# The last tile of an output projection in pieces, the shift of rows moved to GpSimd, and one weight load issued earlier

## What is computed

```python
x = x + g1 * y_x                                        # y_x = (merged branches) @ w_out
hx2 = modulate(rms_norm(x, norm_ffn_g[l]), sh2, sc2)    # h * (1 + scale) + shift
x = x + g2 * grouped_moe(hx2, router_w, router_b, w_exp_gate[l], w_exp_up[l], w_exp_down[l])

# grouped_moe
scores = jax.nn.sigmoid((h @ router_w).astype(jnp.float32))
biased = scores + router_b.astype(jnp.float32)
group_score = lax.top_k(grouped, TOP_K)[0].sum(-1)      # 4 groups of 4 experts, the best group wins
_, idx = lax.top_k(masked, TOP_K)                       # two experts within it
for e in range(N_EXPERTS):
    he = jax.nn.silu(h @ w_gate[e]) * (h @ w_up[e])
    out = out + combine[..., e:e + 1] * (he @ w_down[e])
```

## Time and profile before

| | us |
|---|---|
| median of 3 runs | 1580.73 |
| range of the runs | 1579.6 to 1580.88 |
| the profiled execution, its own time | 1578.25 |
| its span (first to last instruction) | 1576.6 |
| PE busy | 1506.4 (96%) |
| DVE busy | 704.4 (45%) |
| ACT busy | 332.8 (21%) |
| POOL busy | 118.8 (8%) |

### The profile page before, as it was taken

One profiled execution on the slowest core, in us unless ns is written; L12 is line 12 of the kernel. 1 busy time (PEld: TensorE's weight loads), 2 busy tenths in 40 slices (PEclk: granted clock), 3 DMA queues, 4 the chain that ended last, 5 costly groups with the idle time before them and its releaser, 6 DMA issues. The chain is left out here.

```text
span 1576.6 us, 23833 instructions
## 1 busy us (share of the span) xinstructions
PE 1506.4 (96%) x9898; PEld 1023.3 (65%) x9898; DVE 704.4 (45%) x1420; ACT 332.8 (21%) x769; POOL 118.8 (8%) x101
## 2 busy tenths in 40 slices
PE   5999999999999999899999999999999999899995
PEld 2765644766677768775546648786678887655563
DVE  1497777577775442732221135336534312512122
ACT  2121244322223110210101023225322211100001
POOL 0100000032212210000000030000000000000000
PEclk9999999999999999999999999999999999999998
DMA  9575411333544589489999984431134376899997
GB/s 372 203 239 166 156 54 43 119 133 124 158 147 160 173 286 358 173 322 391 400 394 392 402 314 147 138 97 45 38 111 146 121 283 266 343 426 428 419 411 296
DMA packets 128364, 370.24 MB, mean 235 GB/s; under 512 B 14269, under 2 KB 91351, under 8 KB 107516
## 3 DMA queue, kind: packets, MB, share of 16 engines
q1 hardware_dynamic: 118588, 344.86, 58.8%
q10 hardware_dynamic: 5936, 13.09, 2.3%
q0 software_dynamic: 3728, 10.71, 1.9%
HBM read 361.66 MB, written 12.98 MB: 238 GB/s over the span
## 5 line engine op out<-in xcount | busy, mean ns | idle before, releaser
L1247 PE MATMUL ps<-hT,ring 128*128 128x512 f32 (+1 forms) x544 | 207.6, 535 | 0.0
L1250 PE MATMUL ps<-ring,hT 128*128 128x256 f32 (+1 forms) x832 | 173.1, 364 | 3.7 <-DVE arena L2242 2.3
L1250 PEld LDWEIGHTS ps<-ring,hT 128*128 128x128 f32 x832 | 147.0, 190 | 27.5 <-issue 10.3
L1247 PEld LDWEIGHTS ps<-hT,ring 128*128 128x128 f32 x544 | 101.3, 191 | 86.9 <-issue 81.7
L1446 PE MATMUL ps<-arena,ring 128*128 128x512 f32 (+1 forms) x384 | 136.3, 486 | 0.0
L1596 PE MATMUL ps<-arena 128*32 128x128 f32 (+2 forms) x1104 | 102.4, 342 | 0.7 <-DVE arena L2554 0.7
L1596 PE MATMUL ps<-ring,arena 128*64 128x256 f32 (+1 forms) x1280 | 93.9, 334 | 3.8 <-DMA ring<-in_w_exp_gate 2.1
L1446 PEld LDWEIGHTS ps<-arena,ring 128*128 128x128 f32 x384 | 72.4, 190 | 31.7 <-issue 24.6
L2856 POOL DMA_INDIRECT arena<-moe_rows,idx_i x23 | 22.8, 991 | 897.8 <-DVE idx_i L2622 512.9
L1381 PE MATMUL ps<-hT,ring 128*128 128x256 f32 x384 | 87.9, 379 | 0.6 <-ACT arena L1903 0.6
L1159 PE MATMUL ps<-ring,arena 128*128 128x256 f32 x384 | 85.9, 380 | 2.5 <-DVE arena L2420 2.5
(11 more groups left out here) (310 smaller groups left out, 1962.5 us busy)
## 6 DMA issues: line engine op xcount, KB each, us to landing
ring<-in_w_in SPq DMA_DIRECT2D x54, 1024.0 KB, 6.2
ring<-in_w_ada SPq DMA_DIRECT2D x48, 1024.0 KB, 5.3
arena<-in_w_exp_down SPq DMA_DIRECT2D x18, 2048.0 KB, 16.1
arena<-in_w_exp_up SPq DMA_DIRECT2D x15, 2048.0 KB, 15.8
ring<-in_w_exp_down SPq DMA_DIRECT2D x14, 2048.0 KB, 13.7
ring<-in_w_exp_gate SPq DMA_DIRECT2D x12, 2048.0 KB, 16.4
ring<-in_w_exp_up SPq DMA_DIRECT2D x12, 2048.0 KB, 15.0
hT<-in_w_exp_gate SPq DMA_DIRECT2D x10, 2048.0 KB, 15.7
```

The lines of the kernel that those rows point to most:

```text
L1247: last = pe.matmul(ps[:, bank, 0:tok.stop - tok.start], w[:, k, at:at + width], hT[:, k, tok], start=(k == 0), stop=(k == KD - 1))
L1250: last = pe.matmul(ps[:, bank, 0:width], hT[:, k, P * tok:P * (tok + 1)], w[:, k, at:at + width], start=(k == 0), stop=(k == KD - 1))
```

## The change

It has nine parts; the same code serves both layers, so all but the last act twice.

1. The last tile's second half of `w_out` is counted after each quarter. The second quarter goes to the other PSUM bank. DVE mixes 256 columns at a time (`mix(..., piece)`).
2. The first 256 of these columns are turned within the second quarter's product (before its last two steps, `turn_last(0)`), the other 256 after six of the eight router steps (`turn_last(1)`). DVE copies them in two pieces (`keep_last`).
3. The last tile's squares are made over 768 columns and then over 256. The mean of the first part enters the root as its bias (`mean_of_most`).
4. Two small activations call the square root's table and the sigmoid's table ahead of their use.
5. DVE, not ACT, copies the last tile's router strips (`keep_last_parts`).
6. `shift_rows` of all tiles but the last moves to GpSimd. `scale_rows` of these writes into the place of the next tile's row, and its second half for the last but one tile stands behind the first piece of the last tile's mix.
7. The last tile's shift stays on DVE, in halves: column blocks 0 to 3 at its old place, blocks 4 to 7 behind the marks of the slots. PE waits for the first half ahead of the first rows and for the second ahead of column block 4.
8. `keep_busy` has 14 products instead of 10, and three more stand around the last router steps.
9. In the last layer SP issues the gate of expert 2 ahead of the row of tile 3, as the first layer already does.

```diff
-BUSY = (10, 10)
+BUSY = (14, 14)
...
                 first_expert(2)
                 sp.wait_ge(logits, 2 * before(nq, l + 1))
-                if l == 0:
-                    expert_tile(l, 2, 0, 2)
+                expert_tile(l, 2, 0, 2)
                 rows_out(NT - 1)
...
+                            if ends and quarter:
+                                pe.wait_ge(x_mixed, v + l)
+                            bank = 4 + (v + (ends and quarter)) % 2
+                            for k in range(KD):
+                                if ends and quarter and k == KD - 2:
+                                    turn_last(0)
...
-                turn_x(NT - 1, 1)
                 add_parts(NT - 2)
-                router(NT - 1)
+                router(NT - 1, range(6))
+                turn_last(1)
+                keep_busy(2, 1)
+                router(NT - 1, range(6, KD))
+                keep_busy(1, 1)
                 add_parts(NT - 1)
                 keep_busy(BUSY[l])
...
+                mix(NT - 1, 1, 0)
+                keep_x(NT - 2)
+                scale_rows(NT - 2, 1)
+                mean_of_most()
+                keep_last(0)
+                mix(NT - 1, 1, 1)
+                if NT - 3 >= t0:
+                    scale_logits(NT - 3)
+                keep_last(1)
+                scale_logits(NT - 2)
+                keep_last_parts()
+                dve.wait_ge(x_mixed, halves(l, 2 * nq[l] + 1))
+                root_of(NT - 1)
+                scale_rows(NT - 1, 0)
+                scale_logits(NT - 1)
+                scale_rows(NT - 1, 1)
...
-                shift_rows(NT - 1)
+                shift_last(0)
...
                 dve.tensor_tensor(next_slots[:, 0:n, :].rearrange("p t (a q) -> p t a q", a=lists),
...
+                shift_last(1)
...
+            def shift_rows(l, t):
+
+                by_row = lambda a: a.rearrange("p (q k) -> p q k", k=KD)
+                if t > first_tile(l):
+                    pool.wait_ge(h2_ready, turned_halves(l, t - first_tile(l)))
+                pool.wait_ge(consts_made, scalings(l, t - first_tile(l) + 1))
+                pool.tensor_tensor(h_toks[l][:, t, :].rearrange("p (k q) -> p q k", k=KD), by_row(rows_scaled(l, t)),
+                                   by_row(ffn_rows[l][t // XT][1]), ALU.add).then_inc(h2_ready, 1)
```

More of the change, by code:

```diff
@@ L498, in trunk, with scalings, halves, turned_halves @@
         nq = [NT - first_tile(l) for l in range(DEPTH)]
+        def scalings(l, n):
+            return CONSTS + before(nq, l) + n
+        def halves(l, n):
+            return 2 * before(nq, l) + l + n
+        def turned_halves(l, n):
+            return before(nq, l) + l + n
         def roots(l, n):
@@ L830, in multiplied @@
             if kind == "out":
-                return wo_ready, 2 * before(nq, l) + nq[l] * (1 + j // 2)
+                return wo_ready, halves(l, nq[l] * (1 + j // 2) + j // 2)
             return (moe.gate, moe.up, moe.down)[j], EXPERTS * l + max(i for i in range(EXPERTS) if i % WAYS[l][j] == 0) + 1
@@ L1141, in _ @@
                 sp.nop()
-            sp.wait_ge(x_mixed, 2 * before(nq, DEPTH))
-            sp.wait_ge(h2_ready, before(nq, DEPTH))
+            sp.wait_ge(x_mixed, halves(DEPTH, 0))
+            sp.wait_ge(h2_ready, turned_halves(DEPTH, 0))
             sp.wait_ge(moe.gate, EXPERTS * DEPTH - 2)
@@ L1475, in _, with turn_last @@
                         mods_turn(*at)
+                def turn_last(piece):
+                    pe.wait_ge(x_mixed, halves(l, 2 * nq[l] + piece))
+                    if piece:
+                        pe.wait_ge(h2_dve, turned_halves(l, 1))
+                    else:
+                        pe.wait_ge(h2_act, 2 * before(nq, l) + nq[l])
+                    for k in range(2):
+                        last = pe.transpose(ps[:, 0 if piece else nq[l] - 1, P * k:P * (k + 1)],
+                                            res[:, NT - 1, P * (4 + 2 * piece + k):P * (5 + 2 * piece + k)], ident)
+                    last.then_inc(h2_turned, 1)
                 def turn_x(t, half):
-                    pe.wait_ge(x_mixed, 2 * before(nq, l) + nq[l] * half + t - t0 + 1)
+                    pe.wait_ge(x_mixed, halves(l, nq[l] * half + t - t0 + 1))
                     if half:
@@ L1521, in _ @@
                         v = 2 * before(nq, l) + nq[l] * half + t - t0
+                        ends = half and t == NT - 1
                         if v >= 2:
-                            pe.wait_ge(x_mixed, v - 1)
+                            pe.wait_ge(x_mixed, v - 1 + l)
                         for quarter in range(2):
@@ L1531, in _ @@
                             w = kview(n_out + 2 * half + quarter)
-                            last = product(ps[:, 4 + v % 2, COLS * quarter:COLS * (quarter + 1)],
-                                           [(yT[l][k][:, P * t:P * (t + 1)], w[:, k, :]) for k in range(KD)])
+                            if ends and quarter:
[4 more added lines that the diff above has]
+                                    turn_last(0)
+                                last = pe.matmul(ps[:, bank, COLS * quarter:COLS * (quarter + 1)], yT[l][k][:, P * t:P * (t + 1)],
+                                                 w[:, k, :], start=(k == 0), stop=(k == KD - 1))
+                            if ends and not quarter:
+                                last.then_inc(wo_ready, 1)
                         last.then_inc(wo_ready, 1)
@@ L2001, in keep_parts @@
                     act.activation(parts_kept[:, i % 2, :], ps[:, 6, P * i:P * (i + 1)], ACT.Copy).then_inc(h2_act, 1)
+                act.activation(root[:, :], eps[:, :], ACT.Sqrt)
                 for t in range(t0, NT):
@@ L2006, in _ @@
                 for t in range(t0, NT):
-                    squares(ready, junk2, t, t + 1)
+                    if t == NT - 1:
+                        squares_of_most()
                     if t > t0:
                         keep_parts(t - 1)
-                keep_parts(NT - 1)
+                    if t < NT - 1:
+                        squares(ready, junk2, t, t + 1)
+                squares_of_last()
+                act.activation(root[:, :], eps[:, :], ACT.Sigmoid)
                 act.wait_ge(scaled, before(nq, l + 1))
@@ L2536, in _ @@
                         scale_logits(t - 2)
-                    if t == NT - 1:
-                        keep_x(t)
-                        scale_logits(t - 1)
-                        dve.wait_ge(x_mixed, 2 * before(nq, l + 1))
-                    dve.wait_ge(std_ready, roots(l, NT + t - t0 + 1))
-                    step(dve.reciprocal(rstd[:, t:t + 1], rstd[:, t:t + 1]))
+                    root_of(t)
                     if t == t0:
```

115 lines of the change are left out of this document (77 added, 38 removed).

## The result

The changed kernel takes 1584.48 us (median of 16 runs, 1582.43 to 1588.41), the kernel before 1580.88 beside it: ratio 1.0020, 95% interval 1.0013 to 1.0028. It is slower by 3.6 us where the forecast was 6.9 us of gain.

The account below looks back on a forecast made before the run. PE's waits were taken to bound the kernel first, in the last layer the weight stream. Terms 0.9 + 1.3 + 3.2 + 1.5 = 6.9 us gave 1573.8 us against the median of 1580.73; range 1570.5 to 1578.8.

Parts of the forecast that it names:

- the wait gone: First layer, up to the last tile: PE's wait for keep_x at 638.47 disappears, 0.9 us gained.
- the last tile: First layer, last tile: assign ready 0.5 us earlier and the marks 0.8 us earlier still, 1.3 us gained.
- The clock term: First layer: full clock under the first half of the first expert's rows, 3.2 us; rival of low clock 0.27.
- arrives at the end unchanged: What the first layer's passage gives PE was claimed to reach the end in full.
- PE's chain: Last layer: first rows at 1348.4 instead of 1351.31, expert 0's gate done 2.9 us earlier for PE.
- GpSimd's shift: Last layer: tile 2's shift on GpSimd taken as 3.7 us, so its row goes 1.95 us later.
- The lower bound: Last layer: the least time taken for GpSimd's shift of tile 2, 2.35 us.
- DVE is slowed by GpSimd: Rival, both layers: one slowed DVE step in each costs 1.0 us; about 1578.5, no measurable change; chance 0.10.
- I take 7: Last layer: expert 1's gather assumed to land in 7 us, between 4.9 on idle queues and 8.3 on full ones.
- The term of +1.5: Last layer, weight stream: 1.5 us gained by filling idle DMA time, bounds −0.4 and 3.2.
- the third gate costs the gather: Rival, last layer: gather as slow as 8.3 us, term −0.4, sum 5.0, 1575.7 us; chance 0.12.

Follow-up runs that it names:

- e1: The changed kernel with part 9 undone: 1579.07 us, ratio 0.9982 to the kernel before.
- e7: The kernel before, with the last layer's gate of expert 4 asked for behind expert 1's up product, not its gate product: 1583.71 us, ratio 1.0016.
- e3: The changed kernel with the last layer's row of tile 3 issued from ScalarE's (ACT's) queue, not SP's: 1587.03 us, ratio 1.0033 to the kernel before.
- e9: The changed kernel with its new 8-byte tile allocated behind arena, not ahead of it: 1585.46 us, ratio 1.0026 to the kernel before.
- e14: Parts 1 to 8 alone, with the new tile allocated behind arena: 1577.27 us, ratio 0.9972 to the kernel before.
- e4: The changed kernel, with the last layer's gate of expert 3 held until expert 1's gathered rows arrive: 1581.06 us, ratio 0.9997 to the kernel before.
- e6: Parts 1 to 8 without part 9, the last layer's gate 3 held until expert 1's gathered rows land: 1579.91 us, ratio 0.9997 to the kernel before.
- e2: The kernel before with part 9 alone: 1580.77 us, ratio 0.9995 to the kernel before.

## Why the prediction was wrong

**First layer: right at the first gate product, not in what arrives.** Forecast 5.4 us, traced 5.5 there, with all three terms as worked out: the wait gone (0.93), the last tile 1.4 to 1.5 us sooner (1.3 forecast), the clock at full speed under the first rows (3.2). The clock term was in part a matter of the execution: 10 of 11 had it, e1 had not. The working also read 0.11 us per transpose out of four in 0.6 us, which give 0.15; the 28 filling records then took 3.37 us against 3.3 forecast, so nothing hung on it. What failed is "arrives at the end unchanged": rows that come sooner are wanted sooner, and 1.1 us went to two waits for gathers. T lies 698.7 to 700.9 us behind the first event in the ten profiled kernels with parts 1 to 8 whose first rows ran at full clock, and 703.0 to 706.3 in the five with the old passage, 4.3 us by the means; against the kernel before and e7 alone (703.6 and 703.7), which had no second stretch of low clock, it is 3.8 us. Where the rest of the 5.5 went in the kernels without the two waits is open.

**Last layer, PE's chain: right.** 2.9 us forecast, 3.2 traced.

**GpSimd's shift: mis-sized, without harm.** Its line, after:

```profile
1334.95 2.37 POOL L3022 TENSOR_TENSOR arena<-arena,ret_tab 128x1024 f32<-128x1024 f32 x1 [396.28 <-DVE ss_most L2545]
```

I multiplied the contiguous 2.35 us by DVE's 1.59 for the regrouping; on GpSimd it costs nothing. The lower bound was the value, and the row of tile 2 goes 0.5 us later, not 1.95. The rival "DVE is slowed by GpSimd" stayed small: in these two passages one DVE step is longer than its like, the add of the last layer's second piece (0.67 us at 1336.93, while POOL's sum ends, against 0.42 at 1333.18), and it is 0.67 to 0.69 in all twelve kernels with parts 1 to 8. That is 0.25 us, not 1.0 in each layer; its cause was not tested.

**Last layer, the weight stream: here it failed.** On a clock that starts at T, I had the last row landed at 21.6 and the gather issued at 21.7: it was 22.0 and 22.9. Then "I take 7", with 8.3 as the worst: it was 10.4. The 8.3 of rows 10 was measured with gate 3 asked for 3.9 us behind the gather; the working itself put gate 3 ahead of it, with up 3 close behind, and kept the old bound all the same. PE got the rows at T + 33.3 instead of 28.7. From there the working went on at full clock, where the longer wait brought 0.50 and 2.6 us more. Gate 4 was asked for at T + 41.2, not at 34.0, and the stream stood empty for 8 us, not 1.9. So the step that failed is the landing time of the gather, and with it its worst case. The term of +1.5, bounds -0.4 to 3.2, came out below its lower bound: in the two traces the stretch from T to the end grew by 10.7 us, and part 9 alone is some -6 by the medians (the change against e1). Of the rivals "the third gate costs the gather" named the place; it had the term fall from +1.5 to -0.4, a price of 1.9 us where some 6 came. The rule of the Trainium skill cited there (DMA: Bandwidth & Descriptors, Queues, rings and completion order) gave the direction, but e3 shows that the row is delayed from another queue as well, so it is not the ring's order that this trace bears out.

**Not in the sum at all: the new tile.** The rate of the weight stream was taken as given. 8 bytes in part 3 took 1.2% of it, worth 2.7 to 2.8 us in the kernel before; with parts 1 to 8 it is 1.6 at overlapping intervals, and in the change as it stands nothing was measured (e9).

The shares are these, by the ratios. Parts 1 to 8 with `arena` in place gain 4.4 us (e14), about what the first layer has at T. From there one way leads over e1: the shift of `arena` costs 1.6 and part 9 another 6.0. The other leads over e9: part 9 costs 8.5, and the shift of `arena` then changes it by -0.9, within the intervals. Both end at the 3.2 us of loss because each step is a difference of two runs, so the sum proves nothing by itself. What both ways show is that part 9, put on top of parts 1 to 8, costs 6 to 8.5 us, more than they gain.

The range of times lay too low for the same reason: its upper end rested on bounds from rows in which the load beside the gather was lighter than the change would make it.

## What to carry to other kernels

- A landing time read from a trace holds for what else was asked for around it. Before using it as a bound, list the requests that the changed kernel has outstanding at that moment; a small transfer on which the next request hangs wants the big ones cut or held, not merely another queue. Half a load ahead of such a transfer did no harm where a whole one cost more than the hole was worth, and holding a load back helped only where the wait for it was long (e4, not e6).
- A gain on an engine moves its requests together. Two changes that each gained or did nothing (parts 1 to 8, part 9) lost in company, so price them together at the point where their requests meet.
- A change may add a small tile: look at where the large ones then begin.

## What was unexpected of the hardware

- A gather of 128 rows of 4 KB landed in 4.7 us with nothing beside it (e4) and in 4.6 with the next load asked for 2.6 us behind it (e2), in 5.3 to 9.0 with a load or the rest of one, and in 10.4 to 11.2 with gate 3 and up 3 asked for within 3 us of it. The same gather of the first layer took 4.9 us before and 9.8 after.
- The start of one tile, 32 bytes off a multiple of 256, took the weight stream from 421 to 416 GB/s.
- Like code ran at a granted clock of 0.50 (the lower level, 1.2 GHz) in some executions and at 1.00 in others at the same place (3.81 or some 7 us for 32 records).
- GpSimd took 2.37 us for a regrouping sum of 1024 columns, as for a contiguous one (2.35); DVE takes 1.94 and 1.22 for the same two.
